# Expert up matrices read in runs of 16384 bytes, and the experts' norm scales read in the first stage

## What is computed

```python
def hier_moe(h, w_grp, b_grp, w_rt, b_rt, w_up, w_down):
    # h = rms_norm(hidden, moe_norm): scaled by a gain per channel
    g_prob = softmax(xt @ w_grp + b_grp)            # 4 groups, the best one is taken
    e_logit = (xt @ w_rt + b_rt)[best group]        # 8 experts in it, the best two are taken
    gate = softmax(e_val) * g_gate
    # each token goes to its two experts:
    gate_up = xb @ w_up[e]                          # 1024 x 1024
    a, u = split(gate_up, 2)
    y = (silu(a) * u) @ w_down[e]                   # 512 x 1024
    # h = h + sum of the two results, each times its gate
```

## Time and profile before

| | us |
|---|---|
| median of 3 executions | 2739.46 (2737.55 to 2743.38) |
| profiled execution, whole time | 2746.47 |
| its span, first to last instruction | 2744.5 |
| TensorE busy | 2500.6 (91%) |
| VectorE, ScalarE, GpSimd busy | 1095.6, 600.9, 579.7 |
| DMA queue q1 (issued by SP), share of 16 engines | 46.1% |

### The profile page before, as it was taken

The page is one execution under the profiler, slowest core; times in us unless marked ns, Lnnn a source line. Parts: engine busy times, 40 slices in busy tenths (PEclk is TensorE's granted clock), DMA queues, the critical chain, the costliest instruction groups (busy, mean ns, idle before and its releaser), DMA issues. The chain is left out here.

```text
span 2744.5 us, 38635 instructions
## 1 busy us (share of the span) xinstructions
PE 2500.6 (91%) x15450; PEld 1392.2 (51%) x15450; DVE 1095.6 (40%) x2071; ACT 600.9 (22%) x1420; POOL 579.7 (21%) x714
## 2 busy tenths in 40 slices
PE   7997899889989999998999999869898889999995
PEld 4554446645544444545555555358455455554442
DVE  4636544553255554754111211153556541111112
ACT  2217022232211222811001000023355111000100
POOL 1834333271124231430000000020444200000001
PEclk9998999988999999999999999989999899999998
DMA  5220103000020411117999999660001089999997
GB/s 181 93 78 31 66 31 112 34 31 2 15 96 9 147 62 67 44 70 275 417 422 422 422 422 422 261 215 32 32 33 63 0 328 422 422 422 422 422 422 292
DMA packets 133367, 532.40 MB, mean 194 GB/s; under 512 B 23600, under 2 KB 33712, under 8 KB 84080
## 3 DMA queue, kind: packets, MB, share of 16 engines
q1 hardware_dynamic: 120624, 505.23, 46.1%
q10 hardware_dynamic: 10240, 16.79, 1.7%
q0 software_dynamic: 2368, 8.52, 0.9%
HBM read 507.27 MB, written 23.10 MB: 193 GB/s over the span
## 5 line engine op out<-in xcount | busy, mean ns | idle before, releaser
L3729 PE MATMUL psum<-arena,hidden_T 128*64 128x512 f32 x1344 | 296.1, 592 | 0.0
L3718 PEld LDWEIGHTS psum<-hidden_T,arena 128*128 128x128 f32 x2304 | 266.8, 192 | 49.6 <-issue 49.6
L3718 PE MATMUL psum<-hidden_T,arena 128*128 128x128 f32 x2304 | 283.3, 278 | 0.0
L3741 PE MATMUL psum<-weight_ring,hidden_T 128*64 128x512 f32 x1024 | 233.8, 598 | 19.7 <-DMA weight_ring<-in_moe_w_down 15.6
L3995 POOL DMA_INDIRECT arena<-expert_rows_out,arena x18 | 20.1, 1118 | 1050.7 <-issue 533.6
L3729 PEld LDWEIGHTS psum<-arena,hidden_T 128*64 128x64 f32 x1344 | 98.8, 137 | 188.6 <-issue 188.6
L3723 DVE TENSOR_TENSOR hidden_T<-psum,arena 128x512 f32<-128x512 f32 x64 | 44.2, 691 | 293.9 <-PE psum L3729 182.7
L3729 PE MATMUL psum<-weight_ring,hidden_T 128*64 128x512 f32 x704 | 155.0, 593 | 0.0
L3865 ACT ACTIVATE hidden_T<-psum 128x256 f32<-128x256 f32 x64 | 24.5, 383 | 526.6 <-PE psum L3729 526.6
L3741 PEld LDWEIGHTS psum<-weight_ring,hidden_T 128*64 128x64 f32 x1024 | 69.6, 137 | 137.7 <-issue 119.5
L4272 PE MATMUL psum<-weight_ring,hidden_T 128*128 128x512 f32 x256 | 124.9, 619 | 0.0
(11 more groups left out here) (629 smaller groups left out, 4315.1 us busy)
## 6 DMA issues: line engine op xcount, KB each, us to landing
arena<-in_moe_w_up SPq DMA_DIRECT2D x84, 2048.0 KB, 18.4
weight_ring<-in_moe_w_down SPq DMA_DIRECT2D x64, 2048.0 KB, 16.5
weight_ring<-in_moe_w_up SPq DMA_DIRECT2D x44, 2048.0 KB, 16.4
weight_ring<-in_hg_w_in SPq DMA_DIRECT2D x8, 2048.0 KB, 10.5
weight_ring<-in_ev_w_in SPq DMA_DIRECT2D x8, 1536.0 KB, 8.8
weight_ring<-in_fox_w_in SPq DMA_DIRECT2D x6, 2048.0 KB, 11.1
weight_ring<-in_od_w_in SPq DMA_DIRECT2D x5, 2048.0 KB, 8.3
weight_ring<-in_ple_w_gate SPq DMA_DIRECT2D x4, 2048.0 KB, 9.1
```

The source lines that it names most:

```text
L3718: last = nc.tensor.matmul(g.psum[:, c // 4, (c % 4) * P:(c % 4 + 1) * P], keep[:, i, c * P:(c + 1) * P], row[:, i, :], start=i == 0, stop= ...
L3729: last = nc.tensor.matmul(g.psum[64 * q:64 * q + 64, 2 + n, :].rearrange("p (s c) -> p s c", s=2), xT[:, k // 4, k % 4, ROWS * n:ROWS * n ...
L3741: last = nc.tensor.matmul(g.psum[64 * q:64 * q + 64, 6 + n, :], aT[:, k % 2, 64 * (k // 2):64 * (k // 2) + 64], down[b][:, k, 512 * q:512 ...
```

## The change

The up matrices are read with four neighbouring rows of 4096 bytes to a partition, so that a run in memory is 16384 bytes; a half (512 rows) is then exactly one such run for each of 128 partitions. The down matrices stay at 8192 bytes. The channel order follows: the router's weights, the permuted copy on ScalarE (now a step of four elements where it was two) and the norm scales. The norm scales of both mixtures are no longer loaded in each routing stage by four DMAs; they get a place in `g.gains` and are loaded once, at the end of SP's list in the first stage, by sixteen DMAs of 32 partitions by 4 elements each. The first stage's load of the other scales is cut to the columns that it still has to bring.

```diff
         self.gains = sb("norm_gains", [P, 6 * KD])
+        self.expert_gains = self.gains[:, 4 * KD:].rearrange("p (layer k j) -> p layer k j", layer=2, j=4)
+        self.expert_gains_in = self.sem("expert_gains_loaded")
...
-            sp.dma_start(g.gains[:, :], a["norm_gains"]).then_inc(*gains_in.up(16))
+            sp.dma_start(g.gains[:, 0:4 * KD], a["norm_gains"][:, 0:4 * KD]).then_inc(*gains_in.up(16))
             sp.wait_ge(*zeroed.at(1))
             sp.dma_start(g.h[0:META, 0, :], a["meta_tokens_2"]).then_inc(*meta_in.up(16))
             g.feed(sp, ring_upto)
             sp.wait_ge(*meta_in.at(16))
+            gains = a["norm_gains"][:, 4 * KD:6 * KD].rearrange("p (k quarter) -> p k quarter", quarter=4)
+            placed = g.expert_gains.rearrange("p layer k j -> p (layer k) j")
+            for quarter in range(4):
+                for j in range(4):
+                    sp.dma_start(placed[32 * quarter:32 * quarter + 32, :, j], gains[j::4, :, quarter], allow_slow_non_contiguous=True).then_inc(g.expert_gains_in, 16)
...
     def load_up(self, sp, e, n, half):
-        return sp.dma_start(self.up[n][:, 4 * half:4 * half + 4, :].rearrange("p (k j) f -> p k (j f)", j=2), self.wu[bass.ds(e, 1)].rearrange("a (two k p j) f -> two p (a k) (j f)", two=2, p=P, j=2)[half])
+        return sp.dma_start(self.up[n][:, 4 * half:4 * half + 4, :].rearrange("p j f -> p (j f)"), self.wu[bass.ds(e, 1)].rearrange("a (two p j) f -> two p (a j f)", two=2, p=P, j=4)[half])
...
-        self.gain = g.take(4, 2)
-        self.gains = g.a["norm_gains"][:, (4 + layer) * KD:(5 + layer) * KD].rearrange("p (k two) -> p k two", two=2)
-        self.loaded, self.gain_in = g.sig("router_loaded", "gains_loaded")
+        self.gain = g.expert_gains[:, layer]
+        self.loaded = g.sig("router_loaded")
...
-        for side in range(2):
-            for j in range(2):
-                sp.dma_start(self.gain[64 * side:64 * side + 64, :, j], self.gains[j::2, :, side], allow_slow_non_contiguous=True).then_inc(*self.gain_in.up(16))
-        for j in range(2):
-            sp.dma_start(w[:, j::2, 0:GROUPS], a["moe_w_grp_2"][n].rearrange("(k p j) n -> j p k n", p=P, j=2)[j], allow_slow_non_contiguous=True).then_inc(*self.loaded.up(16))
-            sp.dma_start(w[:, j::2, GROUPS:], a["moe_w_rt_2"][n].rearrange("(k p j) n -> j p k n", p=P, j=2)[j]).then_inc(*self.loaded.up(16))
+        for k in range(2):
+            sp.dma_start(w[:, 4 * k:4 * k + 4, 0:GROUPS], a["moe_w_grp_2"][n][512 * k:512 * k + 512].rearrange("(p j) n -> p j n", j=4), allow_slow_non_contiguous=True).then_inc(*self.loaded.up(16))
+            sp.dma_start(w[:, 4 * k:4 * k + 4, GROUPS:], a["moe_w_rt_2"][n][512 * k:512 * k + 512].rearrange("(p j) n -> p j n", j=4)).then_inc(*self.loaded.up(16))
...
-    by_pairs = lambda ap: ap.rearrange("p (k r j) -> p k j r", k=4, j=2)
-    in_order = lambda ap: ap.rearrange("p (k j r) -> p k j r", k=4, j=2)
+    by_fours = lambda ap: ap.rearrange("p (k r j) -> p k j r", k=2, j=4)
+    in_order = lambda ap: ap.rearrange("p (k j r) -> p k j r", k=2, j=4)
...
-                nc.scalar.activation(in_order(keep[0:n, i, :]), by_pairs(g.h[0:n, t, :]), ACT.Copy, scale=rs[0:n, i:i + 1]).then_inc(*scaled.up())
+                nc.scalar.activation(in_order(keep[0:n, i, :]), by_fours(g.h[0:n, t, :]), ACT.Copy, scale=rs[0:n, i:i + 1]).then_inc(*scaled.up())
...
-            dve.wait_ge(*router.gain_in.at(64))
+            dve.wait_ge(g.expert_gains_in, 256)
```

## The result

The changed kernel takes 2748.06 us (median of 20 runs, 2742.44 to 2753.12); the kernel before, run 20 times beside it, 2743.53 us (2737.55 to 2746.85). The ratio is 1.0014, with a 95% interval of 1.0008 to 1.0021: slower by 0.14%, some 4 us, and the interval, 2.2 to 5.8 us, doesn't hold zero. I had predicted no change, -0.3 us, and 2739.2 us within 2731 to 2747, so the time lies 1.1 us outside. Of the 8.9 us between 2739.2 and 2748.06, 4.1 are that the three runs shown before had a median of 2739.46 where twenty have 2743.53; the other 4.8 are the 4.5 between the two medians of twenty and my -0.3. The first part is the chance of three runs, the second is the change's.

What follows compares the result with a forecast made beforehand. TensorE was taken to bound all but the second mixture's later part, which reads bound. Gains 3.2 + 3.7 + 1.0 = 7.9 us, costs 4.6 + 3.0 = 7.6, net -0.3: 2739.46 to 2739.2 us, range 2731.0 to 2747.0.

Steps and rivals of the forecast that it cites:

- What bounds the kernel: Expert stages: TensorE sets the first mixture's pace (15.33 us an expert), reads that of the second's later part (15.52 us).
- The price of a long run: Up-matrix reads: 614.4 ns per 16384-byte packet against 621.2 for two of 8192; 0.109 us an expert, 3.2 us in all.
- the restart: Second mixture: reads start again when expert 0's up product is done and expert 3's up matrix is issued; then they end the stage.
- reads that pay nothing: Rival, chance 0.22: the long run is cut or 422 GB/s is a ceiling; the 3.2 us are missing, 2742.4 us.
- slow long packets: Rival, chance 0.09: in the second mixture a 16384-byte packet takes 634 ns; net +8.8, 2748.3 us.
- The first stage: End of SP's list: sixteen DMAs at 0.68 us delay TensorE by 4.6 us, a slow clock costs 3.0; together 7.6.
- The routing stages, the scales gone: Four scale DMAs gone per routing stage: gains of 1.0 us in the first mixture, 3.7 in the second.
- the wait of 2.6: Second mixture's routing stage: TensorE's idle time for the router's last load goes, gaining 2.6 us.
- the clock's second fall: Second mixture's routing stage: TensorE's clock no longer falls to half after that idle time, 1.7 us more.
- At nothing: Parts expected to cost nothing, among them ScalarE's permuted copy at a step of four; at worst 0.1 us per routing stage.
- three signs that I had named for being wrong: Sixteen issues ending before 20.6 us, a 16384-byte packet over 621 ns, or a changed pace in the first mixture.

Runs made afterwards that it cites:

- run 20: Not a label but part of "run 20 times": the kernel before, unchanged, measured beside the changed kernel; median 2743.53 us.
- order of four: Changed kernel with the up matrices read as before and the sixteen scale DMAs issued at the end of the second stage's list; 1.0004 against the kernel before.
- the step table: Kernel before with extra 128x1024 copies in its first stage, on ScalarE, VectorE and GpSimd at several steps; run once, 2753.45 us.

## Why the prediction was wrong, step by step

**What bounds the kernel**: right. The first mixture's pace is unchanged at 15.33 us with reads at 427 GB/s, and only the second's later part got faster.

**The price of a long run**: right in kind; the size per packet too small, and the total right partly by luck. The median packet of 16384 bytes takes 614 ns by the trace's records, the 614.4 that the rows gave; 16,384 of them replace twice as many, and with 128 small ones more the page counts 16,256 fewer, 117111. But by the same records a packet of 8192 bytes took 313 ns before, not 310.6, so a long one saves 12 ns and not 6.8, and an expert's pace fell by 15.52 - 15.35 = 0.17 us, not 0.109. TensorE gained 3.5 us in the second mixture of after (from a lag of 3.49 us at its first up product to 0.04 at its last down product) and 4.1 in the kernel with the long reads alone, for my 3.2. The Trainium skill's estimate by its DMA page (DMA: Bandwidth & Descriptors, "Why small descriptors are slow") was 1.6 us; the trace shows more than twice that, and the measurement decides. Twenty-nine experts at 0.17 would be 4.9 us. The records of the landings tell where the rest is: from the up matrix of expert 3 to that of expert 31 they show 435.2 us before, 431.3 after and 431.5 with the long reads alone, 3.8 to 3.9 us or 0.14 an expert. The first matrices behind the restart came no closer together than before; from about expert 8 on each is 0.16 us faster. The rivals of reads that pay nothing and of slow long packets both fell.

**The first stage**: the sum right by luck, since its two parts are off in opposite directions. I said 4.6 us of delay and 3.0 of slow clock, 7.6 together. The opening came 6.2 us later (27.06 against 20.84 for SP's next DMA), the upper end of my bounds, and the half clock until about 31 us cost 1.8: 8.0 us. Nor does all of the 1.8 surely belong to the change: in the kernel with the scales out at a step of two, and in that with every second copy on VectorE, nothing delays the opening, TensorE is idle for 1.97 us, and still the granted clock fell to 0.50 for some 3.4 us just behind it and cost 1.6 us. The mis-sized term is the sixteen issues: not 0.68 each, but 0.57 each and 4.0 once, on the first. I had taken SP to be free at 14.32 us because its issues of weights had ended there; it was free to hand over, but the next issue still took 4 us.

**The routing stages, the scales gone**: the kernel with a step of two shows what this part is worth. In the second mixture TensorE is 4.27 us earlier, where I had 4.3, the wait of 2.6 and the clock's second fall of 1.7; both went, as reasoned. Of this 3.5 us are left at the last down product (the lag is -3.38 us at the routing stage's start and -6.88 there), near my 3.7: the reads took the rest, as reasoned too. In the first it is 3.07 against the profile of before, past my bounds of 0.7 to 2.4, but 2.2 against the two other executions of the same routing stage (19.26 and 19.22 us), within them; either way my 1.0 was too low. And in the execution with the first-stage edit alone the second mixture's wait was not there to be won. So this part is 4.7 us by the ratio, as forecast, but between 3.1 and 7.3 by single executions.

**"At nothing"**: this is the step that failed. I wrote of ScalarE's permuted copy, "I expect no change; should a step cost as much again, a tenth of a us in each routing stage". The row I had, 1.14 us at a step of two, is that of an access which is as fast as one in order, and says nothing of a step of four. A price that no row shows has to be bounded from both sides, so a doubling belonged at the far end: 1.14 us more on the first copy, which TensorE waits for in both stages, and as much on each next one where TensorE is the faster. Measured, a copy takes 0.92 us more, TensorE starts later by that, waits between tiles, and its clock stays at half for longer: 4.0 us in the first mixture and 2.3 in the second. With these 6.2 us my net would have been +5.9, just above the 2.2 to 5.8 that were measured; with the scales' gain of 7.3 that the profile of before gives, and not 4.7, it would have been +3.3.

**The sum again**, with measured terms: first stage +8.0; first routing stage +1.0; second -2.0; reads -3.5 to -4.1; net +2.9 to +3.5 us, against 4 (2.2 to 5.8) measured. That it fits so well is partly chance: the terms are differences from one execution of before, whose routing stages were up to 0.9 and 3.4 us longer than others of the same code. The three parts as separate kernels add up too: first stage 0.21%, long reads -0.09%, order of four 0.04%, together 0.16% against 0.14%, where each of the three is known to 0.1% only.

**A number that fits for the wrong reason.** The rival of slow long packets named 2748.3 us, and 2748.06 was measured. Its mechanism did not happen: the packets took 614 ns and not 634. And none of the three signs that I had named for being wrong came: the sixteen issues ended at 26.67 and not before 20.6, no packet of 16384 over 621 ns at the median, the first mixture's pace 15.33. I had named no sign for the copy, since I had put it at nothing.

**What stays open.** In the profiled execution of after, TensorE's products lag 8.0 us behind those of before from the second stage on, and only 1.4 us at 1240 us; in the kernel with the first stage's edit alone the lag shrinks in the same way, from 8.8 to 5.1 us there, 4.3 by the first mixture and nothing by the second. Yet the medians keep most of it (5.8 us by that kernel's ratio). The other kernels explain this. Between 200 and 1240 us all of them run the same code, and the lag shrinks in each: by 3.5 to 6.6 us in the three that open the second stage late, and by 0.2 to 5.5 us in the seven that don't (the step table, with its added work, left out). The kernel with its scales in the second stage, never delayed, goes from -0.5 to -4.1 us. So the shrinking is no giving back of the delay; the execution of before that was profiled was itself slow there (its whole time is 2.9 us above the median of its twenty, that of after 0.9 below). The granted clock falls to half at idle times that come at other moments and last otherwise in each execution: in before also from 1186.0 to 1189.4 us, where after has full clock. So a single profile can't give the sum of a change as small as this. What the first stage costs lies between 3.3 and 8.2 us by the one comparison of times, 6.9 in the middle of the other; the 6.2 us of delay can't be told from the 8.0 by them. Why the router's last load sometimes lands in 3.1 us and mostly in 5 is open, too.

## What to carry to other kernels

A change of the order in which data lie in memory reaches every access that must follow the order: list them all, and price each at its own step, not at the step it had. A gain in bytes per run is small once runs are 8 KB (0.17 us of 15.5 here), and small things around it, sixteen tiny DMAs at a place where everybody waits, eat it up. Put such loads where SP has time, as at the end of the second stage's list: the same sixteen take SP 12.6 us at either place, and cost the kernel up to 8 us ahead of the second stage and nothing that the times show behind it. And before a difference of a few us between two profiles is put down to a change, look at the same place in other executions of code that wasn't changed there: here a stage of 18.6 us differed by 3.4.

## What the runs showed of the hardware that I had not expected

- ScalarE's copy of 128x1024 f32 between on-chip buffers costs 1.15 to 1.22 us at read steps of one or two elements and 2.13 to 2.19 at four or eight; with reads in order and writes 128 elements apart 2.15 (1.90 from one to the next in a routing stage, where a step of four has 2.06). VectorE makes the copy at a step of four in 1.16 us.
- A small DMA behind three chunks of weights on the same queue holds SP for 4.0 us, the ones behind it for 0.57 each; behind two chunks, at the end of the second stage, the first holds it for 3.0. The end of SP's issues isn't yet the time from which SP is free.
- The clock falls in the first 50 us too: TensorE was idle for 8.48 us ahead of 27.11, and the granted clock was 0.53 (nearly the level of 1.2 GHz) for the four microseconds around its start. It came back sooner there than behind the shorter idle time of the earlier trace rows. In two other executions it fell at that place behind an idle time of 1.97 us, and in that of before, with 1.65 us, it didn't.
